# Half of a Q projection moved inside its attention, values' products left behind the transposes of their step

## The reference, cut to what matters

```python
def mixer_a(x, w_qkv, b_qkv, sinks, w_o, b_o, cos, sin):
    B, S, _ = x.shape
    nq, nkv = A_HEADS * HEAD_DIM, A_KV_HEADS * HEAD_DIM
    qkv = x @ w_qkv + b_qkv
    q = apply_rope(qkv[..., :nq].reshape(B, S, A_HEADS, HEAD_DIM), cos, sin)
    k = apply_rope(qkv[..., nq:nq + nkv].reshape(B, S, A_KV_HEADS, HEAD_DIM), cos, sin)
    v = qkv[..., nq + nkv:].reshape(B, S, A_KV_HEADS, HEAD_DIM)
    o, _ = block_attention(q, k, v, WIN_BLK, A_WINDOW - 1, True, sinks)
    return o.reshape(B, S, nq).astype(x.dtype) @ w_o + b_o
...
    for i in range(DEPTH):
        kind, j = i % N_MIXERS, i // N_MIXERS
...
        x = layer_norm(DN_ALPHA * x + h, ln_g[i, 0], ln_b[i, 0])
        x = layer_norm(DN_ALPHA * x + swiglu(x, w_gate_up[i], w_down[i]), ln_g[i, 1], ln_b[i, 1])
```

## Time and profile before

| | us |
|---|---|
| median of 3 runs (lowest, highest) | 2402.16 (2400.73, 2404.18) |
| profiled execution, its own time | 2401.17 |
| its span | 2399.0 |
| TensorE busy | 2354.6 (98%) |
| VectorE busy | 1636.2 (68%) |
| ScalarE busy | 1137.8 (47%) |
| POOL busy | 225.4 (9%) |
| granted TensorE clock, mean | 1.000 |

### The profile page before, as it was taken

The page is one execution under the profiler, slowest core; times in us unless marked ns, Lnnn a source line. Parts: engine busy times, 40 slices in busy tenths (PEclk is TensorE's granted clock), DMA queues, the critical chain, the costliest instruction groups (busy, mean ns, idle before and its releaser), DMA issues.

```text
span 2399.0 us, 31702 instructions
## 1 busy us (share of the span) xinstructions
PE 2354.6 (98%) x12768; PEld 1980.5 (83%) x12768; DVE 1636.2 (68%) x2282; ACT 1137.8 (47%) x1523; POOL 225.4 (9%) x238
## 2 busy tenths in 40 slices
PE   7999999999999999998999999999999999999999
PEld 6788888887888778886888888888888888988887
DVE  7766755557667676677776777777676577687664
ACT  5543345554433544435443455564444365574442
POOL 2400002012000220003100100100100001001000
PEclk9999999999999999999999999999999999999999
DMA  6465343335553455643754344444755344445652
GB/s 250 143 204 207 141 176 141 141 141 176 202 202 141 176 176 193 211 147 122 263 195 174 137 176 159 158 177 148 280 187 182 119 162 158 174 176 186 226 173 91
DMA packets 259072, 418.97 MB, mean 175 GB/s; under 512 B 11984, under 2 KB 149200, under 8 KB 258928
## 3 DMA queue, kind: packets, MB, share of 16 engines
q1 hardware_dynamic: 254064, 400.15, 47.1%
q0 software_dynamic: 4864, 16.80, 2.2%
HBM read 415.86 MB, written 1.05 MB: 174 GB/s over the span
## 4 chain that ended last, share of the span: by engine, by line
PE 89%; DVE 5%; ACT 2%; DMA 1%; issue 1%; POOL 0%; SPq 0%; DVEq 0%; ACTq 0%
PE bank_L L2561 19%; PE bank_L L2577 16%; PE bank_S L2981 8%; PE bank_T L2946 7%; PE bank_L L2946 7%; PE bank_O L2981 7%; PE bank_L L2558 4%; PE bank_T L2951 4%; PE bank_L L2951 4%; PE bank_S L2577 1%; DVE wlo L1715 1%; PE bank_S L2561 1%; PE bank_O L2561 1%; PE bank_T L2528 1%; PE bank_T L2516 1%
## 5 line engine op out<-in xcount | busy, mean ns | idle before, releaser
L1715 DVE TENSOR_TENSOR wlo<-raw,whi 128x2048 fp32r<-128x2048 f32 x316 | 717.5, 2290 | 119.6 <-ACT whi L1292 119.1
L1292 ACT ACTIVATE whi<-raw 128x2048 fp32r<-128x2048 f32 x290 | 542.3, 1894 | 46.8 <-DMA raw<-in_w_in 12.5
L2561 PE MATMUL bank_L<-whi,xt 128*128 128x512 f32 (+2 forms) x1632 | 495.2, 386 | 0.9 <-DVE wlo L1715 0.8
L2577 PE MATMUL bank_L<-whi,xt 128*128 128x512 f32 x1152 | 359.3, 393 | 2.5 <-DVE xt L1729 1.8
L2561 PEld LDWEIGHTS bank_L<-whi,xt 128*128 128x128 f32 x1632 | 296.5, 188 | 57.7 <-issue 2.8
L2561 PE MATMUL bank_L<-wlo,xt 128*128 128x512 f32 (+2 forms) x816 | 311.6, 382 | 0.0
L1587 ACT ACTIVATE tok<-tok 128x256 f32<-128x256 f32 x96 | 40.1, 417 | 449.7 <-DVE tok L2267 449.7
L2577 PEld LDWEIGHTS bank_L<-whi,xt 128*128 128x128 f32 x1152 | 213.3, 188 | 48.0 <-issue 2.7
L2577 PE MATMUL bank_L<-wlo,xt 128*128 128x512 f32 x576 | 225.0, 391 | 0.0
L2946 PE MATMUL bank_T<-xt,whi 128*128 128x512 f32 x768 | 192.4, 393 | 0.0
L2946 PE MATMUL bank_L<-xt,whi 128*128 128x512 f32 x768 | 191.8, 392 | 0.0
(11 more groups left out here) (380 smaller groups left out, 3792.2 us busy)
## 6 DMA issues: line engine op xcount, KB each, us to landing
raw<-in_w_gate_up SPq DMA_DIRECT2D x176, 512.0 KB, 5.5
raw<-in_w_in SPq DMA_DIRECT2D x72, 1024.0 KB, 6.8
draw<-in_w_down SPq DMA_DIRECT2D x44, 1024.0 KB, 6.1
raw<-in_ffn_w_up SPq DMA_DIRECT2D x88, 512.0 KB, 5.6
raw<-in_b_w_qkv SPq DMA_DIRECT2D x36, 1024.0 KB, 7.0
draw<-in_ffn_w_down SPq DMA_DIRECT2D x22, 1024.0 KB, 6.0
raw<-in_w_lift SPq DMA_DIRECT2D x16, 1024.0 KB, 6.5
raw<-in_a_w_qkv SPq DMA_DIRECT2D x12, 1024.0 KB, 8.3
```

The costliest lines, as they stand in the source:

```text
L1292: act.activation(wide(whi, w, nkc, ncols)[:, ks, :], wide(raw, w, nkc, ncols)[:, ks, :], ACT.Copy) \
L1715: dve.tensor_tensor(wide(wlo, w, nkc, ncols)[:, ks, :], wide(raw, w, nkc, ncols)[:, ks, :], wide(whi, w, nkc, ncols)[:, ks, :].bitcast(F32 ...
L2561: mm = pe.matmul(banks[name][:, 0:st["ncols"]], xx[:, kk, t * P:(t + 1) * P], ww[:, kk, :], start=(kk == 0 and q == 0), stop=(kk == nkc - ...
L2577: mm = pe.matmul(banks[bank][:, :], xx[:, k, t * P:(t + 1) * P], ww[:, k, :], start=(k == 0 and q == 0), stop=(k == KC - 1 and q == 2))
```

## The change

In layers 0 and 3 the second half of Q becomes a fill: 5 k-steps, the turns of K and of the first half, 3 k-steps, and the other 8 in steps 0 to 5 of the attention, 1, 1, 2, 1, 1, 2. Its rotation is in VectorE's step 6, its turn on TensorE in step 7, ahead of the values' products. The fill takes bank L1, so scores have S0 and S1 alone. The values' products stand at the same steps 5, 7, ... 19 and directly behind the transposes, as before (`late=False`). The first half of w_o's weights is split ahead of the attention, subtractions stand at steps 3, 10 and 18, POOL's four casts behind its scalings of heads 2, 3, 5 and 6, and 10 k-steps of the output product inside, at steps 10, 14, 16 and 18, not 8 at 16 to 18. The biases lie in `pts` and `sm`, which the attention overwrites, and the row for the second half of Q in `r`, loaded by a transfer of its own; those of layer 3 but this row are loaded in layer 2. In layers 1 and 2 fills, subtractions and pieces of the output product stand at other steps.

```diff
@@ -157,6 +155,7 @@
...
+        abias, abo, bias_q = pflat, smflat[:, 0:D], r[:, 1, 0:NW]
...
@@ -456,6 +455,11 @@
...
+        def biases(j, after):
+
+            add("abias", j=j, after=after)
+            n["inn"] += 2
...
@@ -518,16 +522,20 @@
...
+            values = {}
+            for j in range(len(units) // 2):
+                at = 2 * j + lag + 2
+                values[at + 1 if late and at < len(units) else at] = j
+            last_of = sorted(values)[1::2]
+            st = add("spread", units=units, ready=ready, first=first, to=to, lag=lag, lead=lead, fill=fill, qb=SB if fill else QB,
+                     values=values, late=late, needs=needs or {}, ropes=ropes or {}, turns=turns or {}, pool_highs=pool_highs or {},
...
@@ -612,8 +627,10 @@
                 qT = blk(0, 2048).rearrange("p (h s) -> p h s", s=SEQ)
                 kT = blk(2, 1024).rearrange("p (h s) -> p h s", s=SEQ)
                 vv = blk(3, 512).rearrange("p (t c) -> p t c", t=T)
-                add("abias", j=j, after=[x_is if i == 0 else (down_done, n["d"])])
-                n["inn"] += 2
+                if i == 0:
+                    biases(j, [x_is])
...
@@ -629,15 +646,22 @@
                 k_ok = rope(heads(tks[0]), 8, 0, is_in[0])
                 pair_end()
                 q_ok = rope(heads(tks[1]), 8, 0, is_in[1])
-                turn(tks[0], k_ok, kT)
+                v_ok = (dev, n["dev"])
                 add("exp_table")
                 add("biased_rows", inn=n["inn"])
                 tk = next_tok()
-                linear(lhs, a_cols(1), NW, "bias", tk=tk, c=1, v=vv, inn=n["inn"])
-                ok = rope(heads(tk), 8, 0, (dev, n["dev"]))
+                late = linear(lhs, a_cols(1), NW, "bias", tk=tk, c=1, v=vv, inn=n["inn"])
+                late["kind"], late["span"], w1 = "fill", (-1, 0, 6), late["w"] + 1
+                ok = (dev, n["dev"])
+                part(late, 0, 5)
+                turn(tks[0], k_ok, kT)
                 turn(tks[1], q_ok, qT[:, 0:4], by=BY)
+                add("high_ahead", w=w1)
+                add("low_ahead", w=w1, half=0)
                 first = (turn_done, n["turn"])
-                behind = [turn(tk, ok, qT[:, 4:8], by=BY)]
+                part(late, 5, 8)
+                rope_in, ok = rope(heads(tk), 8, 0, ok, inside=True)
+                turn_in = turn_inside(tk, ok, qT[:, 4:8], by=BY)
                 units = []
                 for h in range(16):
                     kv, rows = h // 4, []
@@ -649,11 +673,13 @@
-                pool_splits([n["w"] + 1])
-                att = spread(units, [(turn_done, n["turn"]), (dev, n["dev"])], first, behind, to[0], 3, 5, 400,
-                             lows={18: (n["w"] + 1, (0,))}, parts={16: [(0, 0, 0, 2)], 17: [(0, 0, 2, 4)], 18: [(1, 0, 0, 4)]},
-                             rest=[(0, 0, 4, 6), (0, 1, 0, 6), (0, 0, 6, 8), (0, 1, 6, 8), (1, 0, 4, 8), (1, 1, 0, 4), (1, 1, 4, 6),
-                                   None, (1, 1, 6, 8)])
+                hi_by_pool.add(w1 + 1)
+                att = spread(units, [v_ok], first, to[0], 3, 5, 400, fill=[late], late=False, needs={8: (turn_done, n["turn"])},
+                             ropes={6: rope_in}, turns={7: turn_in}, pool_highs={2: (w1 + 1, 0), 5: (w1 + 1, 1)},
+                             lows={3: (w1, (1,)), 10: (w1 + 1, (0,)), 18: (w1 + 1, (1,))},
+                             parts={10: [(0, 0, 0, 2)], 14: [(0, 0, 2, 4)], 16: [(1, 0, 0, 4)], 18: [(0, 0, 4, 6)]},
+                             rest=[(0, 1, 0, 4), (0, 0, 6, 8), (0, 1, 4, 8), (1, 0, 4, 8), (1, 1, 0, 4), (1, 1, 4, 6), None,
+                                   (1, 1, 6, 8)])
...
@@ -690,7 +716,7 @@
-                                               ["L0", "L0"])
+                                               [["L0", "O0"], ["L0", "L0"]])
...
@@ -737,11 +763,11 @@
-                        att = paired(pairs, first, to=to[1], fill=[(sts[0], (0, 1, 2)), (sts[1], (2, 3, 5))],
-                                     splits={0: (w1, (0,)), 1: (w1, (1,)), 4: (w1 + 1, (0,)), 6: (w1 + 1, (1,)),
-                                             9: (w1 + 2, (0, 1))},
-                                     parts={6: [(0, 0, 0, 2)], 7: [(0, 0, 2, 4)],
-                                            8: [(0, 0, 4, 6), (0, 1, 0, 4), (1, 0, 0, 2)], 9: [(0, 1, 4, 6), (1, 0, 2, 4)]}, **banked)
+                        att = paired(pairs, first, to=to[1], fill=[(sts[0], (0, 0.5, 1)), (sts[1], (1, 3, 5))],
+                                     splits={0: (w1, (0,)), 1: (w1, (1,)), 3: (w1 + 1, (0,)), 8: (w1 + 1, (1,)),
+                                             9: (w1 + 2, (0,))},
+                                     parts={5: [(0, 0, 0, 2)], 6: [(0, 0, 2, 4)], 7: [(0, 0, 4, 6)],
+                                            8: [(0, 1, 0, 4), (1, 0, 0, 2)], 9: [(0, 1, 4, 6), (1, 0, 2, 4)]}, **banked)
...
@@ -797,11 +823,11 @@
-                             fill=[(late[0], (0, 0.5, 1)), (late[1], (1, 2, 3)), (late[2], (3, 4, 6))], ropes=ropes_, turns=turns_,
+                             fill=[(late[0], (0, 0.5, 1)), (late[1], (1, 2, 3)), (late[2], (3, 4, 5))], ropes=ropes_, turns=turns_,
-                             parts={6: [(0, 0, 0, 2)], 7: [(0, 0, 2, 4)], 8: [(0, 1, 0, 4), (1, 0, 0, 2)],
-                                    9: [(1, 0, 2, 4), (0, 0, 4, 6), (0, 1, 4, 6)]})
+                             parts={5: [(0, 0, 0, 2)], 6: [(0, 0, 2, 4)], 7: [(0, 1, 0, 2)],
+                                    8: [(0, 1, 2, 4), (1, 0, 0, 2), (0, 0, 4, 6)], 9: [(1, 0, 2, 4), (0, 1, 4, 6)]})
...
@@ -813,6 +839,8 @@
+            if i + 1 < DEPTH and (i + 1) % 3 == 0:
+                biases((i + 1) // 3, [(pv_done, n["pv"])])
...
@@ -1217,27 +1270,27 @@
...
                         pool.tensor_scalar(smflat[:, q], smflat[:, q], rl[:, k % 4, 1:2], None, ALU.mult).then_inc(scaled_2, 1)
+                        for e in range(2):
+                            if i - e in st["pool_highs"]:
+                                high(*st["pool_highs"][i - e], e)
...
+                elif st["kind"] == "bias_q":
+                    for s_, v in st["after"]:
+                        pool.wait_ge(s_, v)
+                    pool.dma_start(bias_q, a_b_qkv[st["j"], NW:2 * NW].partition_broadcast(P)).then_inc(rows_full, 16)
                 elif st["kind"] == "load_mem":
                     for s_, v in st["after"]:
                         pool.wait_ge(s_, v)
@@ -1499,14 +1552,18 @@
                             exps(i)
                         if 1 <= i <= len(U):
                             scales(i - 1)
-                        if i > lag and (i - lag) % 4 == 0:
-                            group_high(to, at["pv"], (i - lag) // 4 - 1)
+                        if i in st["ends"]:
+                            group_high(to, at["pv"], st["ends"][i])
+                        if i in st["turns"]:
+                            heads_hi(st["turns"][i])
                         if i in st["highs"]:
                             split_hi(*st["highs"][i])
-                        for late, t in ends(st["fill"], i - 1, st["steps"]):
+                        for late, t in inside_ends(st["fill"], i - 1, st["steps"]):
+                            if late["evac"] == "act":
+                                evacuated(late, t, LB[t])
+                    for late, t in inside_ends(st["fill"], st["steps"] - 1, st["steps"]):
+                        if late["evac"] == "act":
                             evacuated(late, t, LB[t])
-                    for late, t in ends(st["fill"], st["steps"] - 1, st["steps"]):
-                        evacuated(late, t, LB[t])
                 elif st["kind"] == "attention":
                     U = st["units"]
 
@@ -1818,7 +1875,8 @@
-                    dve.tensor_tensor(st["tk"][:, t, :], ps[:, :], abias[:, c0:c0 + NW], ALU.add).then_inc(dev, 1)
+                    row = (abias[:, 0:NW], bias_q)[st["c"]]
+                    dve.tensor_tensor(st["tk"][:, t, :], ps[:, :], row, ALU.add).then_inc(dev, 1)
...
@@ -2115,13 +2175,18 @@
                             reciprocal(i - 1)
-                        if i > lag + 1 and (i - lag - 1) % 4 == 0:
-                            group_low(to, (i - lag - 1) // 4 - 1)
+                        if i - 1 in st["ends"]:
+                            group_low(to, st["ends"][i - 1])
                         if 0 <= i - lag < len(U):
                             copies(i - lag)
+                        for late, t in inside_ends(st["fill"], i - 1, st["steps"]):
+                            if late["evac"] == "bias":
+                                biased(late, t, LB[t])
+                        if i in st["ropes"]:
+                            rotated(st["ropes"][i])
                         if i in st["lows"]:
                             split_lo(*st["lows"][i])
-                    group_low(to, len(U) // 4 - 1)
+                    group_low(to, len(to["dst"]) - 1)
```

(18 more changed lines are left out.)

70 lines of the change are left out of this document (44 added, 26 removed).

## The result

The changed kernel takes 2421.93 us (median of 4, 2421.26 to 2422.49), the one before 2401.89 (median of 4, 2400.73 to 2404.18): 1.0082 times as long, 95% interval 1.0065 to 1.0100. The forecast was 2407.9, with a range of 2399 to 2414. The profiled execution has a span of 2419.2 us, with a mean granted clock of 0.993 where it was 1.000.

A forecast was written before the change was run, and what follows sets the result against it. TensorE, busy 98% of the span, was taken as the bound. Terms 9.2 + 1.0 − 3.5 − 1.0 = +5.7 on the profiled 2401.17 gave 2406.9, with the median 1.0 higher 2407.9; range 2399 to 2414.

The forecast's parts named there:

- scores of 2 and 3: Attention with sinks, first half: with two banks they wait for reductions behind the subtraction put ahead, 2.8 us idle.
- The turn: Step 7, second Q half: TensorE waits 2.5 us for VectorE's rotation, then 0.9 for a bank for its second half.
- The values of heads 0 and 1: Attention with sinks, first half: wait 1.75 us for head 1's copy, behind step 3's subtraction and head 4's reductions.
- Those of 4 and 5: Attention with sinks, second half: values still wait about 1.1 us as before, named as a sign to look for.
- per layer +4.6: Each attention with sinks (layers 0 and 3): +5.1 first half, −0.4 and −0.1 second half; two layers +9.2 us.
- The falling clock: Rival, chance 0.07: the 2.8 us idle at step 2 lowers the clock in both layers, +4.8, about 2413 us.
- the walk: Step-by-step reckoning of layer 0's attention at the old run's clock, chaining VectorE end to end; scores of 8, 9 start 68.7.
- From both sides +1 to +7: Per layer with sinks: +1 if the three subtractions inside fall into VectorE's gaps, +7 if casts slow them to 2.9.
- The biases: Layer 3: the second Q half's row is transferred once x is ready, +1.0 us (0 to +2); layer 0: 0.
- Layers 1 and 2: Moved fills and output k-steps remove waits: layer 1 −3.5 us (−4.4 to −1.5), layer 2 −1.0 (−2 to −0.5).
- Halved banks: Scores in attention with sinks: two banks suffice by 0.1 us in plain rhythm; charged only where a subtraction lies between.
- the rival's 2 us per layer: Rival, chance 0.10: step 3's subtraction waits for a whole POOL cast, 2 us once per layer, 2411.9 us.

The follow-up runs named there:

- the clock held: Changed kernel plus useless transposes keeping TensorE busy at four waits of each attention with sinks: 2415.46 us.
- late values and the two waits mended: Changed kernel with no subtraction ahead of the attention, rotation and turn a step earlier, and values' products one step later: 2406.08 us.
- the third bank alone: Changed kernel with the scores of heads 8 to 15 going round three banks (L1, S0, S1): 2427.53 us.
- the fastest kernel: Changed kernel with nothing subtracted ahead, rotation earlier, values late, bias row apart, third bank from head 8, step 10's subtraction at step 15: 2392.47 us.

## Why the prediction was wrong

- **Waits and their places: right in the main.** Forecast and seen in layer 0: scores of 2 and 3, 2.8 and 2.60; scores of 8 and 9 on ScalarE, 1.7 and 1.68; scores of 12 and 13, 1.4 and 1.22; values of 8 and 9, 1.3 and 1.21. The turn waited 3.40, not 2.5, and its second half 0.16, not 0.9. The values of heads 0 and 1, 1.75, were 0.95 in layer 0 and 2.06 in layer 3. Those of 4 and 5 waited 0.51 and not the 1.1 that was named as a sign. Up to the end of the last values, idle time grew by 3.7 us in layer 0 and by 5.2 in layer 3 (there counted from behind the slow k-steps of the bias wait): 8.9 together, where the two terms of +4.6 had 9.2 in all. That the sum fits is partly luck, since slow matmuls also take up waits; with the clock held they were longer.
- **The clock: the step that failed.** The sum's term "per layer +4.6" was walked in full-speed matmuls, "in the clock of the old run"; it measured 10.1 and 10.0. The falling clock stood beside it as a rival with a chance of 0.07, at 2.4 us for one fall per layer behind one idle. In layer 0 it fell behind the wait at step 2 and behind that at step 7, in layer 3 behind those for the bias row, for the first values (2.06) and for the turn (3.41), and the matmuls of the two attentions took 6.4 and 4.8 us longer. At least 6.5 us of the time are this inside the attentions (run with TensorE busy), and 1.6 more the k-steps behind the bias wait: about 8 of the 20. The trace of before had shown idles of 1.2 to 1.5 us without a fall and one of 5.45 with it; the walk's own 2.8 and 2.5 lay between, next to other idles, and I priced them like the short ones. The Trainium skill, "TensorE: Matmul & The Clock Gate", section "Why this matters for your kernels", warns of idle gaps between bursts of matmuls, but the gaps it means are longer than the one here: behind 2.60 us of idle the clock went to 0.50. Where the two differ, the measurement decides.
- **The term "per layer +4.6": too small without the clock too.** With the clock held, the last values of layer 0 start at 93.79, which is 6.5 us per layer by the same reckoning. The 1.9 us more arise in the first half: scores of 2 and 3 start at 50.87 (50.3 in the walk), values of 0 and 1 at 58.74 (57.9), the turn at 66.26 (64.4), scores of 8 and 9 at 70.82 (68.7). One part is the cast that holds up the rotation by 0.8; the rest was not taken apart. The two places behind most of the loss are shown: with the subtraction and the rotation moved, 16.6 us go.
- **"From both sides +1 to +7" and the range to 2414** held neither, since the far end (+7) added slower subtractions and not a slower TensorE, and the upper bound left out the far end of the falling clock.
- **The biases:** +1.0 forecast, 1.43 of wait more, and 1.6 of slow k-steps behind it, which the term had not.
- **Layers 1 and 2:** −4.5 forecast, −2.7 measured alone, with an interval that just holds the forecast. The two waits of layer 1 became one on transposes (1.1), which I had counted as hidden.
- **Halved banks:** I charged them only where a subtraction lies between, and that was right in this kernel. With late values and the two waits mended, all pairs of scores from heads 6 and 7 on waited on reductions (6.7 us in layer 0), so the Trainium skill's advice ("Perfetto Trace Analysis", "Optimizing Tensor Performance") to rotate through more banks would seem to bind; but the third bank alone did not free TensorE: in the changed kernel the wait went to the transposes. Moving VectorE's subtraction did, with the third bank in place. That VectorE's pace is under both is the likely reading; the same move with two banks would test it.
- **The lock between VectorE and POOL:** the rival's 2 us per layer did not come as one wait. I took 2.03 us for a cast from the sum of four (8.12). Read one by one in the trace before, the casts at 43.16 and 50.24 took 1.04, and those at 44.15 and 47.20 took 3.09 and 3.10, each ending some 0.9 us behind the end of a subtraction (46.35 and 49.39); the subtractions that began during a cast took 2.77 and 3.12 instead of 2.28. So each engine waited for the other's instruction to end. After the change the casts took 1.04, and a rotation step that began within one was held to its end. The Trainium skill's "SBUF — State Buffer", section "Who interferes with whom", calls this an exclusive lock in which the order of issue decides who waits, and the trace agrees.

## What to carry to other kernels

When work is moved so that TensorE will wait longer than the waits that left the clock alone before (up to 1.5 us in the layers here; falls came behind single waits of 1.67 us and more, and behind several short ones), walk the matmuls behind it at the low clock, too, and give that a fair chance. Before filling gaps of the bound engine, ask what the next engine does at that place: in the fastest kernel the subtraction's place on VectorE was worth more (6.1 us) than the place of the values (3.3), and taking the bias row apart gained about as much as the fills of two layers, if not more (3.8 and 2.7). When an edit takes away one of two long waits, try both together as well: only with both did the kernel come back to the time of before.

## What the runs showed that I had not expected

A wait's length alone did not tell whether the clock falls. A single idle of 2.60 us brought it down to 0.50 in layer 0, while the same one in layer 3, ended at 1118.48, was followed by matmuls at full speed (0.73 per pair at 1119.33); there it fell behind the next wait, of 2.06. In the kernel with the third bank alone, which is the same program up to head 8, the same 2.60 in layer 0 left it at 1.00 (52 to 56 us). In the kernel with late values and the two waits mended, the 2.92 us for the bias row left it at 1.00 too. Taking one wait away can thus move a fall instead of removing it, and a third bank, meant to help, went with one more. POOL's cast of 128x1024 takes 1.04 us alone and 3.1 when a subtraction of VectorE is in its way, and the subtraction is held up by a cast as well, so both engines pay for that meeting.
